# Gated delta rule: gate products between the chunk preparations, one block inverse over four chunks, values and keys solved before the state chain

## The reference, cut to what matters

```python
g = jnp.cumsum(g, axis=-1)
decay = exp(where(tri, g[..., :, None] - g[..., None, :], -inf))
a_kk = where(strict, einsum("bnhcd,bnhed->bnhce", k * beta, k) * decay, 0.0)
lhs = a_kk + eye(CHUNK)
rhs = concatenate([v * beta, k * beta * exp(g)], axis=-1)
u, w = split(triangular_solve(lhs, rhs, lower=True, unit_diagonal=True))
a_qk = where(tri, einsum("bnhcd,bnhed->bnhce", q, k) * decay, 0.0)
q_dec, k_dec = q * exp(g), k * exp(g[-1:] - g)
def step(state, inp):                
    v_new = u_c - w_c @ state
    o_c = q_c @ state + a_c @ v_new
    state = state * exp(g_last) + k_c.T @ v_new
```

## Time and profile before

| | |
|---|---|
| time, median of 3 runs | 3148.96 us (3148.87 to 3150.55) |
| the profiled execution's own time | 3136.92 us |
| its span (first to last instruction) | 3135.1 us |
| TensorE busy | 2745.1 us, 88% |
| VectorE, ScalarE, GpSimd busy | 40%, 34%, 29% |
| mean granted TensorE clock | 0.938 of 2.4 GHz |

### The profile page before, as it was taken

The page is one execution under the profiler, slowest core; times in us unless marked ns, Lnnn a source line. Parts: engine busy times, 40 slices in busy tenths (PEclk is TensorE's granted clock), DMA queues, the critical chain, the costliest instruction groups (busy, mean ns, idle before and its releaser), DMA issues. The chain is left out here.

```text
span 3135.1 us, 36399 instructions
## 1 busy us (share of the span) xinstructions
PE 2745.1 (88%) x12748; PEld 2137.3 (68%) x12748; DVE 1253.1 (40%) x2081; ACT 1059.1 (34%) x1513; POOL 894.9 (29%) x379
## 2 busy tenths in 40 slices
PE   5888859899998989998999989666877999899997
PEld 3666637678876766666888857566644888677875
DVE  7699932555445325644111153443110221251112
ACT  3255443422224225554322246111332222242331
POOL 1223203234342200012443424000300444334442
PEclk9999979999999979999999989778887999999998
DMA  5344402355553110011332312000200233222321
GB/s 225 101 161 163 154 29 90 121 174 187 174 166 103 55 41 21 15 35 56 105 98 90 101 54 88 7 1 1 74 7 10 93 113 103 85 74 94 101 93 54
DMA packets 65676, 275.71 MB, mean 88 GB/s; under 512 B 7296, under 2 KB 7552, under 8 KB 57760
## 3 DMA queue, kind: packets, MB, share of 16 engines
q1 hardware_dynamic: 54576, 202.18, 19.6%
q10 hardware_dynamic: 10992, 72.03, 6.4%
HBM read 272.02 MB, written 2.16 MB: 87 GB/s over the span
## 5 line engine op out<-in xcount | busy, mean ns | idle before, releaser
L262 POOL TENSOR_TENSOR w_lo<-raw,w_hi 128x1024 fp32r<-128x1024 f32 x375 | 894.7, 2396 | 2199.2 <-ACT w_hi L254 2199.0
L254 ACT ACTIVATE w_hi<-raw 128x1024 fp32r<-128x1024 f32 x375 | 385.6, 1051 | 464.1 <-PE G L273 172.7
L273 PE MATMUL STAT_G<-h_hi,w_hi 128*128 128x512 f32 x928 | 372.1, 401 | 15.8 <-DVE tn L1669 6.0
L273 PE MATMUL G<-h_hi,w_hi 128*128 128x512 f32 (+1 forms) x944 | 374.1, 396 | 8.9 <-DVE tn L1669 3.2
L273 PE MATMUL G<-h_lo,w_hi 128*128 128x512 f32 (+1 forms) x944 | 368.8, 391 | 0.0
L273 PE MATMUL G<-h_hi,w_lo 128*128 128x512 f32 (+1 forms) x944 | 368.7, 391 | 0.0
L273 PE MATMUL STAT_G<-h_lo,w_hi 128*128 128x512 f32 x928 | 363.9, 392 | 0.0
L273 PE MATMUL STAT_G<-h_hi,w_lo 128*128 128x512 f32 x928 | 363.9, 392 | 0.0
L273 PEld LDWEIGHTS STAT_G<-h_hi,w_hi 128*128 128x128 f32 x928 | 175.9, 190 | 57.2 <-issue 15.8
L273 PEld LDWEIGHTS G<-h_hi,w_hi 128*128 128x128 f32 (+1 forms) x944 | 177.4, 188 | 52.5 <-issue 5.9
L273 PEld LDWEIGHTS G<-h_lo,w_hi 128*128 128x128 f32 (+1 forms) x944 | 177.4, 188 | 38.5 <-issue 1.7
(11 more groups left out here) (395 smaller groups left out, 3835.3 us busy)
## 6 DMA issues: line engine op xcount, KB each, us to landing
raw<-in_units SPq DMA_DIRECT2D x375, 512.0 KB, 3.4
mod_w<-in_modw ACTq DMA_DIRECT2D x48, 1024.0 KB, 4.8
mod_first<-in_modw ACTq DMA_DIRECT2D x8, 1024.0 KB, 21.8
acsb<-acs ACTq DMA_DIRECT2D x16, 512.0 KB, 3.6
cw<-in_cw ACTq DMA_DIRECT2D x2, 2048.0 KB, 7.4
x<-in_x SPq DMA_DIRECT2D x1, 2048.0 KB, 12.0
out<-x SPq DMA_DIRECT2D x1, 2048.0 KB, 6.2
const<-in_const SPq DMA_DIRECT2D x1, 1084.0 KB, 16.6
```

What stands on the lines that cost most here:

```text
L254: act.activation(w_hi[s][:, :], raw[s][:, :], ACT.Identity).then_inc(hi_done, 1)
L262: pool.tensor_tensor(w_lo[s][:, :], raw[s][:, :], w_hi[s][:, :].bitcast(F32), ALU.subtract).then_inc(lo_done, 1)
L273: ins = pe.matmul(out[0:m, :], a[s][:, k * P:k * P + m], b[:, c], start=(n == 0 and q == 0), stop=(n == len(blocks) - 1 and q == 2))
```

## The change

1. The unit `gdn_ab` moves from the end of the projections to their front: it is paired with the first unit. The chain of decays runs on VectorE and ScalarE between the convolutions. Its sigmoid is now written as Exp, an addition and `reciprocal` on VectorE.
2. The 4 gate units each stand ahead of one chunk's preparation. Their output is copied, and one SiLU over all four is done later.
3. The preparation is written anew: |d| is taken by ScalarE per head (4 of 128 columns), beta is multiplied in per head, values are scaled by beta and keys by beta*exp(g) as they leave PSUM. Two sets of transposes per chunk are added (`turn_a`, `turn_q`). Level 0 of the inverse needs no matmul any more.
4. Levels 1 to 6 are done for all four chunks together. The mask is applied to q as VectorE takes it out of PSUM. Of x q and q^T x only the half of the columns that changes is formed: the moving operand is 64 of 128 columns, taken as runs of 2 to 64 with gaps. The last level leaves out the x part.
5. Values and keys are multiplied by the inverse ahead of the state chain; a step of the chain is then w S, one subtraction, the state's matmul, one addition.
6. The first `sb` unit stands ahead of the last chunk's outputs, and the four heads' norms stand between units 1 to 5 of `sb`.

The core of the diff:

```diff
+    part("gdn_ab", [("gdn_ab", 0, KC, 0, 36)])
     part("gdn", [(w2, 0, KC, t * P, P) for t in range(12)])
     part("gdn_gate", [(w2, 0, KC, 1536 + t * P, P) for t in range(4)])
-    part("gdn_ab", [("gdn_ab", 0, KC, 0, 36)])
...
+        def half(buf, lv, odd, lo=0, w=T):
+            return buf[:, lo:lo + w].rearrange("p (g two s) -> p g two s", two=2, s=1 << lv)[:, :, odd, :]
+        def packed(buf, lv, lo, w):
+            return buf[:, lo:lo + w].rearrange("p (g s) -> p g s", s=1 << lv)
...
         def gdn_tensor(pe):
-            product_pair(pe, uG, h_hi, h_lo, splits["h_mix2"])
+            product_pair(pe, uA, h_hi, h_lo, splits["h_mix2"], m=(36, P))
+            for t in range(12):
+                if t == 1:
+                    pe.wait_ge(gab, 2)
+                if t >= 2:
+                    pe.wait_ge(gconv, t - 1)
+                if t:
                     product(pe, uG + t, h_hi, h_lo)
                 if 1 <= t <= 8:
                     stat_sums(pe, *norms[f"l2_{t - 1}"], 1)
+                if t == 5:
...
+            def turn_a(c):
+                pe.wait_ge(gprep, 4 * c + 1)
+                pe.wait_ge(gexp, 3 * c + 2)
+                pe.wait_ge(gsub, c + 1)
+                for h in range(4):
+                    ins = pe.transpose(DB[c % 2][:, hb[h]], g_a[c][:, hb[h]], ident)
+            def turn_q(c):
+                pe.wait_ge(gq0, c + 1)
+                for h in range(4):
+                    ins = pe.transpose(DB[c % 2][:, hb[h]], g_qs[c][:, hb[h]], ident)
             for c in range(TT):
+                product(pe, uH + c, h_hi, h_lo)
+                if c:
+                    turn_a(c - 1)
+                pe.wait_ge(gm_done, c + 1)
...
+                if c:
+                    turn_q(c - 1)
+            turn_a(TT - 1)
+            turn_q(TT - 1)
+            for lv in range(1, LEVELS):
+                for c in range(TT):
+                    for h in range(4):
+                        ins = pe.matmul(QB[c][:, hb[h]], g_a[c][:, hb[h]], g_y[c][:, hb[h]], start=True, stop=True)
+                for c in range(TT):
+                    pe.wait_ge(inv_c, n + 1)
+                    for h in range(4):
+                        ins = pe.matmul(packed(UB[c], lv, h * 64, 64), g_x[c][:, hb[h]], half(g_qs[c], lv, 1, h * P, P),
+                    if lv < LEVELS - 1:
+                        for h in range(4):
+                            ins = pe.matmul(packed(UB[c], lv, 256 + h * 64, 64), g_qs[c][:, hb[h]],
+                                            half(g_x[c], lv, 0, h * P, P), start=True, stop=True)
...
+            new_values(0)
+            new_values(1)
+            new_keys(1)
+            new_state(0)
+            new_values(2)
+            new_keys(2)
+            outputs_of(0)
+            state_part(1)
+            new_values(3)
+            new_keys(3)
+            new_state(1)
+            outputs_of(1)
+            state_part(2)
+            new_state(2)
+            outputs_of(2)
+            state_part(3)
+            pe.wait_ge(gw_done, 3)
+            product(pe, at["sb"], h_hi, h_lo)
+            outputs_of(3)
...
+            def decays():
+                v.tensor_scalar(g_row[32:36, 0:T], g_row[32:36, 0:T], 1.0, None, ALU.add).then_inc(gab, 1)
+                v.reciprocal(g_row[32:36, 0:T], g_row[32:36, 0:T]).then_inc(gab, 1)
...
+            for lv in range(1, LEVELS):
+                for c in range(TT):
+                    v.wait_ge(inv_q, n + 1)
+                    v.tensor_tensor(heads(g_qs[c][:, :]), heads(QB[c][:, :]), all_heads(cst("level", lv)),
+                                    ALU.mult).then_inc(inv_c, 1)
+                for c in range(TT):
+                    v.wait_ge(inv_mm, n + 1)
+                    ins = v.tensor_tensor(ys, ys, packed(UB[c], lv, 0, 256), ALU.subtract)
+                    if lv < LEVELS - 1:
+                        ins = v.tensor_tensor(xs, xs, packed(UB[c], lv, 256, 256), ALU.subtract)
...
         def sb_tensor(pe):
-            pe.wait_ge(su_mm, 4)
-            for t in range(12):
+            for t in range(1, 12):
                 product(pe, uS + t, h_hi, h_lo)
+                if t <= 4:
+                    stat_sums(pe, *norms[f"gdn_{t - 1}"], 1)
```

More of the change, by code:

```diff
@@ L1136, in gdn_tensor @@
-                    if c:
[L1137 to L1199, removed]
-                    ins.then_inc(go_mm, 1)
-                    for h in range(4):
-                        b = slice(h * P, (h + 1) * P)
-                        ins = pe.matmul(B5[:, b], g_kd[cc][:, b], g_vn[:, b], start=True, stop=True)
-                    ins.then_inc(su_mm, 1)
@@ L1205, in gdn_tensor @@
-            for h in range(4):
-                stat_sums(pe, *norms[f"gdn_{h}"], 1)
+                    pe.wait_ge(gab, 12)
+                else:
+                    pe.wait_ge(gprep, 4 * c - 1)
+                    pe.wait_ge(gvt, 2 * c)
+                if c >= 2:
+                    pe.wait_ge(gx0, c - 1)
+                pe.matmul(DB[c % 2][:, :], cst("onesf", parts=4), g_m, start=True, stop=True).then_inc(gp_mm, 1)
+                for h in range(4):
+                    ins = pe.matmul(B4[:, hb[h]], piece(g_k, h, c), piece(g_k, h, c), start=True, stop=True)
@@ new lines, in gdn_tensor, with new_values, new_keys @@
+            last = (LEVELS - 2) * TT
+            def new_values(c):
+                pe.wait_ge(inv_done, last + c + 1)
+                for h in range(4):
+                    ins = pe.matmul(QB[c][:, hb[h]], g_y[c][:, hb[h]], piece(g_v, h, c), start=True, stop=True)
+                ins.then_inc(gu_mm, 1)
+            def new_keys(c):
+                for h in range(4):
+                    ins = pe.matmul(UB[c][:, hb[h]], piece(g_k, h, c), g_y[c][:, hb[h]], start=True, stop=True)
+                ins.then_inc(gw_mm, 1)
@@ new lines, in state_part, with new_state @@
+            def state_part(c):
+                pe.wait_ge(gs_done, c)
+                pe.wait_ge(gw_done, c)
+                for h in range(4):
+                    ins = pe.matmul(NRM[:, hb[h]], g_qs[c][:, hb[h]], g_a[c - 1][:, hb[h]], start=True, stop=True)
+                ins.then_inc(ws_mm, 1)
+            def new_state(c):
+                pe.wait_ge(vn_done, c) if c else pe.wait_ge(gu_done, 1)
+                for h in range(4):
+                    ins = pe.matmul(STAT[:, hb[h]], g_kd[c][:, hb[h]], g_x[c][:, hb[h]], start=True, stop=True)
+                ins.then_inc(su_mm, 1)
@@ L1367, in gdn_vector @@
+            state(2)
+            less_state(3)
             for h in range(4):
```

440 lines of the change are left out of this document (258 added, 182 removed).

## The result

The changed kernel takes 2998.59 us in the median of four runs (2997.02 to 3000.07), the kernel before 3148.91 in four runs beside it (3144.54 to 3150.55). The ratio is 0.9532, interval 0.9511 to 0.9552: 150 us less, where 3000 was predicted. The profiled execution of the changed kernel took 2998.98 us, its span is 2997.0.

The account below looks back on a forecast made before the run. The chain across engines and the clock falling in its gaps bound the region. Stages sum to 231.4 against 379.7 us, 148.3 less: 3136.9 goes to 2988.6, plus 12.0 to the median, said as 3000; range 2975 to 3040.

Parts of the forecast that it names:

- The record of 0.111 us: TensorE, float32 matmuls: one record of a 128-column matmul costs 0.111 us, one matmul 0.223; half the columns save nothing.
- the row with one column behind a full weight load: Earlier trace: 33 records with 1 moving column behind a 128-column weight load take 3.5 us, 0.107 each.
- The level of 10.7: Inverse: one level for four chunks is 96 records, 10.7 us on TensorE at the full clock.
- The two rules of the Trainium skill: Inverse: weight load takes 107 ns for 128 columns, or issue gap about 25 ns up to 64, some 19 us shorter.
- with four chunks in turn each wait is covered by the three others: Inverse levels: VectorE's 6.1 us stays under TensorE's 10.7, so TensorE never waits.
- two slow starts of 1.1 us: TensorE after idling in the decays and before the inverse: a slow unit each time, 2 x 1.1 = 2.2 us.
- That 64 columns would hold the clock: Inverse levels: taken at the full clock, as a group with stepped columns held 1.00 for 13 us.
- ScalarE is full in these turns: Projections: the 3.5 us TensorE loses waiting for the Ln behind the decays isn't regained.
- The rival of uncovered gates: Gates and preparations: preparations keep 12.2 us per chunk, units come on top, stage 70.4 not 44.4, kernel 3026; chance 0.10.
- The tail: Behind the last gate unit: the uncovered way through ScalarE and VectorE until the last transposes are through, 9.3 us.
- the rounding in the same queue: ScalarE during gate units: weights' rounding of 1.04 us shares the queue, with only 0.9 us to spare in a turn.
- The single wait: State chain: TensorE waits once, some 1.1 us, ahead of the third `new_state`.

Follow-up runs that it names:

- the last version above: Changed kernel with reciprocal on 128x16, one weight rounding moved behind the preparations, and the last chunk's first level done earlier on VectorE: 2987.08 us, ratio 0.9513.

## Why the prediction was right, and where only its sizes were off

| stage | predicted | measured |
|---|---|---|
| projections | 74.5 | 77.6 |
| gates and preparations | 44.4 | 47.4 |
| inverse | 60.6 | 62.4 |
| state chain and unit | 24.4 | 24.5 |
| norms in units | 25.3 | 25.3 |
| clock, in no stage | 2.2 | in the above |
| sum | 231.4 | 237.2 |

**Unit prices and the inverse.** Right. The record of 0.111 us held at 16, 64 and 128 moving columns, so the row with one column behind a full weight load was the right neighbour. That it is the load which sets this price stays the likeliest reading; it was not varied. The level of 10.7 came out as 10.71, without a gap. The two rules of the Trainium skill ("TensorE: Matmul & The Clock Gate") that were weighed there differ by this: the one on LDWEIGHTS held for these weights of 128 rows, the short gap for up to 64 columns did not show with a full weight load in front. The step "with four chunks in turn each wait is covered by the three others" was right in its result and wrong in its reason: one other chunk covers nearly all (a pair's level takes 5.53 us, of which 5.36 is work), once the way of a level is shorter.

**Clock.** I took two slow starts of 1.1 us. They were 2.1 (the unit behind the Ln wait took 7.6 us, not 5.44) and 1.7 (the first q phase, 5.47, not 3.79), together 3.8 and not 2.2: the row I took the 1.1 from was a single case. In five other executions with the same two waits ahead of the inverse, its first phase took 1.3 to 2.0 us too long, so the 1.7 is one case of several. That 64 columns would hold the clock, as the stepped attention matmuls did, was right, and the 16-column run shows that it wasn't a matter of course.

**Projections.** The mechanism was right, two of its terms were off. The reciprocal was taken at 4.1 from the slope of two short ones and was 3.34. `decays` came to 8.7 and not 7.6, and the wait to 5.1 and not 3.5, since the scans were priced by their duration when alone. The stage is 3.1 longer than the sum said: 1.6 of it the wait and 2.1 the slow unit, less 0.6 in the rest. "ScalarE is full in these turns" was a misreading: the earlier trace rows has it busy for 53.5 of 69.5 us. That the wait isn't regained was right all the same.

**Gates and preparations.** The first turns were right: preparations start 9.8, 10.3 and 10.3 us apart, against 9.9. The rival of uncovered gates is refuted by the run that uncovers them. The tail was priced at 9.3 and took 12.0, 2.0 of the difference by GpSimd's subtraction. The prediction named the rounding in the same queue as a danger; it was not the queue of ScalarE that cost, but the GpSimd operation that it releases.

**State chain and norms.** The stages were right to 0.1. The single wait came where it was forecast, ahead of the third `new_state`, and was 0.84 instead of 1.1.

**From the sum to the median.** This is where two errors met. The region saves 142.5 us and not 148.3. The profiled execution of the changed kernel also came to the region 4.9 us later than that of before, 3.9 of it already at the first residual product (545.6 against 541.7), where no edit reaches; after the region 0.5 came back. So the profiled executions differ by 137.9 and not by 148.3. Against that I added 12.0, the distance of the profiled execution of before to its median, and for the changed kernel this distance is nothing: 2998.98 against 2998.59. The 12.0 was a property of that one execution (its runs spread from 3136 to 3151), not of the kernel. 148.3 less 5.8 less 4.9 plus 0.5 gives 138.1, the difference of the two spans; the medians differ by 150.3. The total of 3000 was therefore hit more closely than the terms deserve, by luck: 5.8 us of the region and 4.9 upstream on the one side, 12.0 on the other. The second comparison of the same two kernels, beside the last version above, gives a smaller saving: 3141.58 less 2999.26 is 142.3 us, which is what the region saved (142.5), and 8 less than the 150.3 of the first. The changed kernel took the same time in both comparisons (2998.59 and 2999.26); the kernel before was 7.3 us slower in the first. Why executions of one kernel differ by several us ahead of the region was not tried and stays open.

## What to carry to other kernels

Before cutting the moving columns of a float32 matmul, look for a row with a full weight load and few columns: if it costs the same, the cut must pay on another engine, and if it goes too far it can cost the clock. In a chain that alternates between engines, first count what stands in the queue between the last subtraction and the next product; the shorter way of a level (the mask moved, the copy gone, the subtractions halved, and with them the clock held) gave far more, 39.6 us, than working on four chunks instead of two, which gave 2. And when a small operation is put on VectorE, ask not only what it takes but whether GpSimd runs at that moment, and what is behind it: taking 3.3 us of reciprocal out of the queue shortened the way to the first preparation by 7.5.

## What the runs showed of the hardware that was not expected

- **VectorE operations on two SBUF operands stood still during GpSimd's subtraction.** 0.69 became 1.44, 2.03 and 2.67 us, by how much of the subtraction was left, and each ended 0.55 us after it. A scan of 0.39 became 2.64. An operation with one operand in PSUM (L1417, 1955.77, 0.69) ran through a subtraction (1955.03 to 1957.39) undisturbed. The Trainium skill ("GPSIMD Engine Reference", Specifications) states it: GpSimd shares its SBUF interfaces with VectorE and contends with instructions that have two SBUF inputs. The trace agrees on both kinds.
- **A TensorE without a gap can fall to its lower level.** With 16 moving columns it was busy 17.40 of 17.40 us at a granted clock of 0.60; with 64, 49.9 of 49.9 us at 1.00.
- **Reads with gaps cost nothing here.** Runs of 2 to 64 columns with gaps between them: 62.4 us for the inverse, and 62.4 with 128 columns in one run.
- **The slow start of the inverse follows neither the last wait nor the last two.** By window, its first 5.2 us in the changed kernel:

```profile
1987.70:1992.90 5.20, 5.20 (x33) 5.20 (x33) 2.70 (x4) 2.12 (x2) 0.00 (x0) 0.66 0.02 5
```

  They ran at 0.66 behind waits of 2.35 and 3.14 us. With waits of 0.37 and 1.86, in the fastest version, the same phase still ran at 0.68 (5.44 us), and with a wait of 3.54, in the version with the gate units first, at 1.00 (3.74 us). The same two waits, 2.35 and 3.14, stand ahead of this phase in the runs with 16 and with 128 columns, with the norms first and with the small reciprocal, and in the changed kernel again. It took 5.09, 5.42, 5.41, 5.75 and 5.06 us there. So it differs by 0.7 us with nothing changed in it. What decides stays open.
